# A different projection group first, its weights loaded in halves, and a norm gain spread by matmuls: the start of a hybrid decoder layer

## The chip, the cores and the metric

The kernel runs on one core of one Trainium2 chip. The metric is the device time of one execution in microseconds, as the median of three runs. Before the change it is 636.16 us (635.68 to 637.22).

## The reference, cut to what matters

One decoder layer on x of 512 tokens by 1024 channels, all in float32:

```
hin = rms_norm(x, norm_g[0])
z   = hin @ w_in                 # 1024 x 2964: moba q,k,v; mLSTM q,k,v,o,i,f; NSA q, six k/v, gates
y   = [moba attention | mLSTM * sigmoid(lo) | NSA attention], each head-normalised
x   = x + rms_norm(y @ w_out, norm_g[1])
hm  = rms_norm(x, norm_g[2])
out = x + rms_norm(relu(hm @ w1)**2 @ w2, norm_g[3])
```

Only the first two lines are touched by the change: the norm of x with its gain row `norm_g[0]`, and the order in which the column groups of `w_in` are multiplied. All groups need the whole normalised and transposed x as an operand.

## The kernel before, in words

**Split numbers.** Every large float32 product is made of three matmuls in the fast float32 format (`mm3`, L1614): high part by high part, high by low, low by high. So each weight chunk and each tile of x is first split: ScalarE copies it into a rounded "high" tile (`ring_h`, `xT_h`), and VectorE or GpSimd subtracts that from the original to give the "low" tile (`ring_l`, `xT_l`).

**Weight chunks.** `w_in` comes in chunks of up to 128 x 2048 elements, numbered by `C_...` (L56). SyncE's queue loads them into two buffers `raw[0]` and `raw[1]` (`load_chunk`, L455; a load waits until the chunk two before it has been split), `high_half(c)` on ScalarE (L672) and `low_half(c)` on GpSimd (L600) split them into a ring of three. For chunks 0 and 1 (`SHARED`) VectorE makes the low part of the first half (`chunk_low`, L1113) and GpSimd that of the second.

**Groups and jobs.** Each column group is one or more jobs `J_...` (L61), and a job fills one of eight PSUM banks (its number modulo 8); `READER` says whether VectorE or ScalarE empties it. TensorE runs in a fixed order (L1686 on): `first_group` (group B: 404 mixed columns, the moba and NSA values and gates), the conv groups LQ and LK, LO, the gate transposes, KV, NQ, the gate columns, LV (512 columns, the mLSTM values), MQ, MK, then the attention parts. A token group such as B, LO and LV has the tokens as stationary operand: 4 token tiles x 8 channel blocks x 3 = 96 matmuls, whose moving operand is 404 columns wide for B and 512 for LO and LV. Its two chunks hold channel blocks 0 to 3 and 4 to 7; below, (t,q) is the 12 matmuls of token tile t with chunk q of the group.

**The start.** SyncE issues, in order: x tile 0, the gain row repeated to all 128 partitions (512 KB), chunk 0, x tile 1, chunk 1, x tiles 2 and 3, small parameters, chunk 2. Chunk B is gathered from four column ranges (pieces of 256, 64, 76 and 8 columns). For each token tile: ScalarE takes the sum of squares and a root (`x_root`, L690), VectorE finishes the reciprocal root and multiplies by the gain (`normalise`, L1106, ending at L1110), TensorE transposes eight 128 x 128 blocks into PSUM (`x_transposes`, L1632), ScalarE copies them to `xT_h` (`x_high`, L697) and VectorE makes `xT_l` (`x_low`, L1120). The queues are written out by hand, and the change leaves this order on the two engines as it is:

```
ScalarE: x_root(0) high_half(0) x_high(0) x_root(1) high_half(1) x_root(2) x_high(1) x_root(3) x_high(2) high_half(2) x_high(3)
VectorE: normalise(0) chunk_low(0) x_low(0) normalise(1) chunk_low(1) normalise(2) x_low(1) normalise(3) x_low(2) x_low(3)
TensorE: x_transposes(0) (0,0) x_transposes(1) (0,1) (1,0) x_transposes(2) (1,1) (2,0) x_transposes(3) (2,1) (3,0) (3,1)
```

`x_low` adds 2 to the semaphore `xl_ready` for each tile, and TensorE waits for 2t+2 before tile t's first matmul.

Of the kernel before, what the change touches and what calls it, by code (L numbers as in the profile page):

```python
# [25 lines left out]
F32 = mybir.dt.float32  # L26
# [40 lines left out]
READER = "vvvv" "vvvv" "aaaa" "v" "v" "a" "a" "aa" "a" "vvvv" "aa" "vv" "aaaa" "vv"  # L67

# [70 lines left out]
def ring_previous(c):  # L139

    if C_WO <= c < C_WO + 3:
        return [C_MQ, C_MK, C_LV + 1][c - C_WO]
    return c - 3 if c < C_CMP else c - 4
# [12 lines left out]
def build(nc, x, norm_g, w_in, conv_w, conv_b, gate_b, cmp_pe, cmp_w1, cmp_w2, head_g, w_out, w1, w2, out):  # L156
    ctx = ExitStack()
    with ctx:
# [144 lines left out]
        small_in = sem("small_in")  # L303
        gain0_in = sem("gain0_in")
        gain1_in, gain2_in, gain3_in = sem("gain1_in"), sem("gain2_in"), sem("gain3_in")
# [53 lines left out]
        def released(c):  # L359

            inside = [C_B, C_LO, C_LV, C_WO, C_WO + 1]
# [92 lines left out]
        def _(sp):  # L454
            def load_chunk(c):  # L455
                if c == C_CMP + 2:
                    sp.wait_ge(silu_done, 4)
                elif c == C_CMP + 3:
                    pass
                elif C_WO <= c < C_WO + RAW:  # L460
                    sp.wait_ge(cmp_used, c - C_WO + 1)
                elif c >= RAW:
                    sp.wait_ge(lo_done, split_no(c - RAW) + 1)
                    if c - RAW in SHARED and raw_slot(c) < RAW:
                        sp.wait_ge(lo_first, SHARED.index(c - RAW) + 1)
                view = grid(raw[raw_slot(c)], c)
                parts = chunk_parts(c)[1]
                k0 = 0
                for j, ((n0, n), src) in enumerate(parts):
                    if C_CMP <= c < C_WO:  # L470
                        dst = view[DH * j:DH * j + DH, :, :]
                    elif C_WO <= c:
                        kk = src.shape[1]
                        dst = view[:, k0:k0 + kk, :]
                        k0 += kk
                    else:
                        dst = view[:, :, n0:n0 + n]
                    sp.dma_start(dst, src).then_inc(raw_in[raw_slot(c)], 16)

# [191 lines left out]
        def _(act):  # L671
# [32 lines left out]
            x_root(0)  # L704
            high_half(0)
            x_high(0)
# [7 lines left out]
            x_high(3)  # L714
            high_half(3)

# [12 lines left out]
            for n in range(4):  # L729
                conv_linear(n)  # L730
                if n >= 1:
                    conv_sigmoid(n - 1)
                if n == 1:
                    high_half(4)
            conv_sigmoid(3)
            high_half(5)
            act.wait_ge(read_v, J_B + NT)
            nc.scalar.activation(gt[:], zB[:, :, BG:BG + 12], ACT.Sigmoid).then_inc(gates_ready, 1)
            high_half(6)
# [3 lines left out]
            high_half(7)  # L743

# [20 lines left out]
            act.dma_start(kwinT[0:DH, :], kwinT[DH:P, :]).then_inc(dup_in, 16)  # L765
            high_half(8)
            high_half(9)
            for p in range(2):
# [5 lines left out]
                                 scale=-1.0).then_inc(read_a, 1)  # L774
            high_half(10)
            high_half(11)
# [288 lines left out]
        def _(dve):  # L1065
# [35 lines left out]

            nc.vector.memset(eps1[:], EPS).then_inc(eps_set, 1)
            link(nc.vector.memset(lv1[:, :, :, DV:DV + 1], 1.0))


            def normalise(t):  # L1106
                link(rsqrt1(SS_X + t, R_X + t, ROOT + t, t + 1))
                if t == 0:
                    dve.wait_ge(gain0_in, 16)
                nc.vector.scalar_tensor_tensor(y[:, t, :], xres[:, t, :], stat[:, R_X + t:R_X + t + 1], gain_a[:],  # L1110
                                               ALU.mult, ALU.mult).then_inc(hn_ready, 1)

            def chunk_low(c):  # L1113
                dve.wait_ge(hi_done, split_no(c) + 1)
# [24 lines left out]


            for t in range(NT):
                dve.wait_ge(job_done, J_B + t + 1)
                nc.vector.tensor_copy(zB[:, t, :], ps[:, (J_B + t) % 8, 0:BN]).then_inc(read_v, 1)
# [469 lines left out]
        def _(pe):  # L1613
# [23 lines left out]


            def first_group():

                pe.wait_ge(consts, 2)
                x_transposes(0)
                for t in range(NT):
                    pe.wait_ge(xl_ready, 2 * t + 2)
                    for q in range(2):
                        wh, wl = chunk(C_B + q)
                        for k in range(4):
                            kk = 4 * q + k
                            last = mm3(ps[:, (J_B + t) % 8, 0:BN], xT_h[:, kk, t * P:(t + 1) * P], xT_l[:, kk, t * P:(t + 1) * P],
                                       wh[:, k, :], wl[:, k, :], kk == 0, kk == NC - 1)  # L1650
                        if q == 1:
                            last.then_inc(job_done, 1)
                        elif t == NT - 1:
                            last.then_inc(part_used, 1)
                        if q == 0 and t < NT - 1:
                            x_transposes(t + 1)

# [414 lines left out]
```

## Time and profile before

| what | value |
|---|---|
| median of three runs | 636.16 us (635.68 to 637.22) |
| the profiled execution's own time | 636.81 us |
| its span, first to last instruction | 635.0 us |
| TensorE busy / share of the chain that ended last | 96% / 89% |
| VectorE, ScalarE, GpSimd busy | 61%, 48%, 39% |

The chain that ended last is the sequence of instructions and waits that leads to the end of the kernel without slack; TensorE's matmuls make nearly all of it. Busy time and the chain are given in shares of the span. Times in the timeline count from the first instruction of the span.

### The profile page before, as it was taken

What the parts mean: (1) busy time and instruction counts of PE and PEld (TensorE: products, weight loads), DVE (VectorE), ACT (ScalarE), POOL (GpSimd) and SP (SyncE); (2) the same over time, 40 slices, a digit from 0 to 9 for tenths busy, and PEclk for the clock granted to TensorE, in tenths of its full rate; (3) what the DMA queues carried; (4) which work ended last, traced back from release to release, by engine and by line L of the source; (5) the groups of instructions that cost most, each with busy time, mean ns of one, the idle gap of its engine ahead of it and who ended that gap; (6) DMA issues with size and microseconds to landing.
All of it is one profiled execution on the core that took longest, in us unless ns stands there. A gap on an engine that the chain in (4) does not pass through costs nothing.

```text
span 635.0 us, 8412 instructions
## 1 busy us (share of the span) xinstructions
PE 606.6 (96%) x3172; PEld 499.2 (79%) x3172; DVE 386.8 (61%) x665; ACT 302.1 (48%) x541; POOL 247.4 (39%) x120
## 2 busy tenths in 40 slices
PE   2999999999989989999999999999999999999995
PEld 2988888886876667889987888888888888888884
DVE  4526031104878877288499968569577595681656
ACT  5415264107566974255563564425545445453422
POOL 4422527402526351005336564172533723812611
PEclk9999999999989989999999999999999999999999
DMA  9442449513240222002704353250340613203002
GB/s 281 136 132 68 132 117 233 127 40 116 85 133 10 59 82 85 1 1 67 266 1 165 101 170 96 76 190 2 133 133 2 211 55 132 67 1 126 40 34 100
DMA packets 45724, 63.50 MB, mean 100 GB/s; under 512 B 6616, under 2 KB 34292, under 8 KB 45684
## 3 DMA queue, kind: packets, MB, share of 16 engines
q1 hardware_dynamic: 45524, 62.71, 32.0%
q8 instruction: 25, 0.41, 0.3%
q10 hardware_dynamic: 160, 0.26, 0.2%
q14 instruction: 15, 0.12, 0.1%
HBM read 58.51 MB, written 2.10 MB: 95 GB/s over the span
## 4 chain that ended last, share of the span: by engine, by line
PE 89%; DVE 5%; ACT 2%; issue 1%; DMA 1%; POOL 1%; SPq 0%; DVEq 0%; ACTq 0%
PE ps L1616 20%; PE ps L1617 19%; PE ps L1618 19%; PE ps L2006 7%; PE ps L2008 7%; PE ps L2007 7%; PE ps L1878 2%; PE ps L1758 1%; PE ps L1863 1%; DMA raw<-in_w_in 1%; PE ps L1782 1%; PE ps L1783 1%; DVE stat L1290 1%; DVE probsT L1302 1%; PE ps L1934 1%
## 5 line engine op out<-in xcount | busy, mean ns | idle before, releaser
L1618 PE MATMUL ps<-xT_h,ring_l 128*128 128x512 f32 (+1 forms) x384 | 143.1, 373 | 0.0
L1616 PE MATMUL ps<-xT_h,ring_h 128*128 128x512 f32 (+1 forms) x384 | 143.0, 372 | 0.0
L1617 PE MATMUL ps<-xT_l,ring_h 128*128 128x512 f32 (+1 forms) x384 | 143.0, 372 | 0.0
L661 POOL TENSOR_TENSOR ring_l<-raw_d,ring_h 128x1024 fp32r<-128x1024 f32 x25 | 67.4, 2707 | 130.8 <-ACT ring_h L931 130.8
L661 POOL TENSOR_TENSOR ring_l<-raw,ring_h 128x1024 fp32r<-128x1024 f32 x31 | 76.8, 2502 | 83.9 <-DVE xres L1459 44.4
L604 POOL TENSOR_TENSOR ring_l<-raw,ring_h 128x2048 fp32r<-128x2048 f32 (+1 forms) x16 | 69.5, 4353 | 85.6 <-ACT ring_h L679 85.6
L1553 DVE TENSOR_TENSOR y<-ps,y 128x512 f32<-128x512 f32 x90 | 61.2, 688 | 52.6 <-PE ps L2008 52.2
L1616 PEld LDWEIGHTS ps<-xT_h,ring_h 128*128 128x128 f32 x384 | 72.6, 189 | 12.9
L1617 PEld LDWEIGHTS ps<-xT_l,ring_h 128*128 128x128 f32 x384 | 72.3, 188 | 12.6
L1618 PEld LDWEIGHTS ps<-xT_h,ring_l 128*128 128x128 f32 x384 | 72.3, 188 | 12.6
L2006 PE MATMUL ps<-ring_h,a_h 128*128 128x512 f32 x196 | 77.4, 395 | 0.0
L2008 PE MATMUL ps<-ring_h,a_l 128*128 128x512 f32 x196 | 77.1, 394 | 0.0
L2007 PE MATMUL ps<-ring_l,a_h 128*128 128x512 f32 x196 | 77.0, 393 | 0.0
L1616 PE MATMUL ps<-ring_h,xT_h 128*128 128x512 f32 (+1 forms) x160 | 62.9, 393 | 3.8 <-POOL ring_l L604 3.8
L1617 PE MATMUL ps<-ring_l,xT_h 128*128 128x512 f32 (+1 forms) x160 | 61.8, 386 | 0.0
L1618 PE MATMUL ps<-ring_h,xT_l 128*128 128x512 f32 (+1 forms) x160 | 61.6, 385 | 0.0
L931 ACT ACTIVATE ring_h<-raw 128x1024 fp32r<-128x1024 f32 x32 | 33.1, 1056 | 23.4 <-PE ps L2008 20.2
L2006 PEld LDWEIGHTS ps<-ring_h,a_h 128*128 128x128 f32 x196 | 36.9, 188 | 8.8 <-issue 0.5
L2008 PEld LDWEIGHTS ps<-ring_h,a_l 128*128 128x128 f32 x196 | 36.9, 188 | 8.6
L2007 PEld LDWEIGHTS ps<-ring_l,a_h 128*128 128x128 f32 x196 | 36.9, 188 | 8.4
L968 ACT ACTIVATE ps<-ps 128x512 f32<-128x512 f32 x32 | 18.7, 583 | 50.1 <-PE ps L1618 50.1
L931 ACT ACTIVATE ring_h<-raw_d 128x1024 fp32r<-128x1024 f32 x32 | 33.5, 1054 | 11.6 <-PE ps L2008 10.8
(248 smaller groups left out, 995.5 us busy)
## 6 DMA issues: line engine op xcount, KB each, us to landing
raw<-in_w_mlp SPq DMA_DIRECT2D x16, 1024.0 KB, 5.4
raw_d<-in_w_mlp SPq DMA_DIRECT2D x16, 1024.0 KB, 6.0
raw<-in_w_in SPq DMA_DIRECT2D x9, 1024.0 KB, 5.3
raw<-in_nsa_cmp_w SPq DMA_DIRECT2D x8, 512.0 KB, 7.2
xres<-in_x SPq DMA_DIRECT2D x4, 512.0 KB, 5.9
raw<-in_w_out SPq DMA_DIRECT2D x2, 1024.0 KB, 6.4
raw<-in_w_out SPq DMA_DIRECT2D x4, 512.0 KB, 4.3
out<-xres SPq DMA_DIRECT2D x8, 256.0 KB, 2.1
```

The lines of the kernel that those rows point to most:

```text
L604: nc.gpsimd.tensor_tensor(ring_l[r][:, n0:n], raw[c % RAW][:, n0:n], ring_h[r][:, n0:n].bitcast(F32), ALU.subtract).then_inc(lo_done, 1)
L661: nc.gpsimd.tensor_tensor(slot(ring_l, n), slot_source(n), slot(ring_h, n).bitcast(F32), ALU.subtract).then_inc(lo_done, 1)
L931: nc.scalar.activation(slot(ring_h, n), slot_source(n), ACT.Copy).then_inc(hi_done, 1)
L968: nc.scalar.activation(tile, tile, ACT.Relu).then_inc(relu_ready, 1)
L1553: nc.vector.tensor_tensor(ya, ps[:, product_bank(b, k) + s, :], ya, ALU.add).then_inc(acc_ready, 1)
L1616: nc.tensor.matmul(o, sh, mh, start=start, stop=False)
L1617: nc.tensor.matmul(o, sh, ml, start=False, stop=False)
L1618: return nc.tensor.matmul(o, sl, mh, start=False, stop=stop)
L1878: last = nc.tensor.matmul(ps[DH * m:DH * m + DH, O_BANK[g], j * P:SEQ], zB[:, j, v0:v0 + DH], block_of(pT[:, g % 2], m, slice(j, NT), j), ...
L2006: nc.tensor.matmul(o, ah, wh[:, q, :], start=fresh and q == 0, stop=not fresh, **go_on)
L2007: nc.tensor.matmul(o, ah, wl[:, q, :], start=False, stop=not fresh, **go_on)
L2008: last = nc.tensor.matmul(o, al, wh[:, q, :], start=False, stop=not fresh or q == 1, **go_on)
```

## The change

It does five things. Group LV moves from behind the gate columns to the front, and B becomes the second group. In `first_group` the order is now (0,0) (1,0) (0,1) (1,1) (2,0) (2,1) (3,0) (3,1), with the transposes of the next token tile still behind each (t,0). Chunk 0 (now contiguous rows of 512 columns) is loaded and copied to its high part in two halves. The gain row is loaded once, as 4 KB, and two matmuls with a row of ones spread it to all partitions in PSUM banks 6 and 7, from where `normalise` reads it. TensorE also makes 10 + 8 + 10 transposes of the identity into an unused bank around these steps. Some of ScalarE's `high_half` calls move earlier in its queue, with the numbers of the chunks shifted, and the parameter transposes go to another bank.

```diff
-C_B, C_LQ, C_LK, C_LO, C_KVS, C_NQ, C_LV, C_MQ, C_MK, C_CMP, C_WO, C_MLP = 0, 2, 3, 4, 6, 7, 8, 10, 11, 12, 16, 20
+C_LV, C_B, C_LQ, C_LK, C_LO, C_KVS, C_NQ, C_MQ, C_MK, C_CMP, C_WO, C_MLP = 0, 2, 4, 5, 6, 8, 9, 10, 11, 12, 16, 20
-J_B, J_CONV, J_LO, J_LI, J_LF, J_KV, J_KS, J_NQ, J_GC, J_LV, J_MQ, J_MK, J_MB, J_H = (
-    0, 4, 8, 12, 13, 14, 15, 16, 18, 19, 23, 25, 27, 31)
+J_LV, J_B, J_CONV, J_LO, J_LI, J_LF, J_KV, J_KS, J_NQ, J_GC, J_MQ, J_MK, J_MB, J_H = (
+    0, 4, 8, 12, 16, 17, 18, 19, 20, 22, 23, 25, 27, 31)
-PARAM_BANK = 7
+PARAM_BANK = 3
+WARM = (10, 8, 10)
...
+                    if c == 0:
+                        sp.dma_start(dst[:, 0:2, :], src[:, 0:2, :]).then_inc(first_in, 16)
+                        dst, src = dst[:, 2:4, :], src[:, 2:4, :]
                     sp.dma_start(dst, src).then_inc(raw_in[raw_slot(c)], 16)
...
-            sp.dma_start(gain_a[:], norm_g[0, 0:1, :].to_broadcast([P, D])).then_inc(gain0_in, 16)
+            sp.dma_start(gain_a[0:1, :], norm_g[0, 0:1, :]).then_inc(gain0_in, 16)
...
             x_root(0)
-            high_half(0)
+            act.wait_ge(first_in, 16)
+            nc.scalar.activation(ring_h[0][:, 0:CHUNK // 2], raw[0][:, 0:CHUNK // 2], ACT.Copy).then_inc(first_hi, 1)
+            act.wait_ge(raw_in[0], raw_full(0))
+            nc.scalar.activation(ring_h[0][:, CHUNK // 2:], raw[0][:, CHUNK // 2:], ACT.Copy).then_inc(hi_done, 1)
             x_high(0)
...
                 if t == 0:
-                    dve.wait_ge(gain0_in, 16)
-                nc.vector.scalar_tensor_tensor(y[:, t, :], xres[:, t, :], stat[:, R_X + t:R_X + t + 1], gain_a[:],
+                    dve.wait_ge(gain0_wide, 1)
+                nc.vector.scalar_tensor_tensor(y[:, t, :], xres[:, t, :], stat[:, R_X + t:R_X + t + 1],
+                                               ps[:, 6:8, :].rearrange("p b n -> p (b n)"),
                                                ALU.mult, ALU.mult).then_inc(hn_ready, 1)
...
+            def warm(n):
+                for _ in range(n):
+                    nc.tensor.transpose(ps[:, 5, 0:P], ident[:], ident[:])
             def first_group():
                 pe.wait_ge(consts, 2)
+                warm(WARM[0])
+                pe.wait_ge(ones_set, 1)
+                pe.wait_ge(gain0_in, 16)
+                for b in range(2):
+                    last = nc.tensor.matmul(ps[:, 6 + b, :], ones_row[:], gain_a[0:1, 512 * b:512 * b + 512], start=True, stop=True)
+                last.then_inc(gain0_wide, 1)
+                warm(WARM[1])
                 x_transposes(0)
-                for t in range(NT):
-                    pe.wait_ge(xl_ready, 2 * t + 2)
-                    for q in range(2):
-                        wh, wl = chunk(C_B + q)
+                warm(WARM[2])
+                for t, q in [(0, 0), (1, 0), (0, 1), (1, 1), (2, 0), (2, 1), (3, 0), (3, 1)]:
+                    if q == 0:
+                        pe.wait_ge(xl_ready, 2 * t + 2)
+                    if t == 0 and q == 0:
+                        pe.wait_ge(lo_first, 1)
+                        wh, wl = grid(ring_h[0], C_LV), grid(ring_l[0], C_LV)
+                    else:
+                        wh, wl = chunk(C_LV + q)
+                    for k in range(4):
+                        kk = 4 * q + k
+                        if t == 0 and kk == 2:
+                            pe.wait_ge(lo_done, 1)
...
             first_group()
+            token_group(J_B, C_B, BN)
...
-            token_group(J_LV, C_LV, 512)
```

## Rows read from the trace of the kernel before

**Rows 1.** The page: engine busy time and the chain that ended last, by engine.

```profile
PE 606.6 (96%) x3172; PEld 499.2 (79%) x3172; DVE 386.8 (61%) x665; ACT 302.1 (48%) x541; POOL 247.4 (39%) x120
...
PE 89%; DVE 5%; ACT 2%; issue 1%; DMA 1%; POOL 1%; SPq 0%; DVEq 0%; ACTq 0%
```

**Rows 2.** TensorE's waits, 0 to 200 us: total us, times, longest.

```profile
PE ps L1635 <- DVE y L1110: 8.1, 1, 8.1
PE ps L1616 <- POOL ring_l L604: 3.8, 1, 3.8
```

**Rows 3.** Timeline of token tile 0: start us, us, engine, line, what.

```profile
1.23 0.29 POOL L578 TENSOR_SCALAR_AFFINE_SELECT ident<-ident 128x128 f32<-128x128 f32 x1 [0.23 <-POOL ident L576]
...
4.22 1.06 ACT L692 ACTIVATE junk<-xres 128x1024 f32<-128x1024 f32 x1 [1.92 <-DMA xres<-in_x]
...
6.64 1.28 DVE L1110 SCALAR_TENSOR_TENSOR y<-xres,stat,gain_a 128x1024 f32<-128x1024 f32 x1
...
8.08 1.94 PE L1635 MATMUL ps<-ident,y 128*128 128x128 f32 x8 [8.08 <-DVE y L1110]
9.34 1.55 ACT L679 ACTIVATE ring_h<-raw 128x1616 fp32r<-128x1616 f32 x1 [3.64 <-DMA raw<-in_w_in]
...
10.80 1.06 ACT L700 ACTIVATE xT_h<-ps 128x512 fp32r<-128x512 f32 x2
...
10.97 2.71 POOL L604 TENSOR_TENSOR ring_l<-raw,ring_h 128x808 fp32r<-128x808 f32 x1 [6.53 <-ACT ring_h L679]
...
13.78 0.68 PE L1616 MATMUL ps<-ring_h,xT_h 128*128 128x404 f32 x1 [3.77 <-POOL ring_l L604]
```

**Rows 4.** Timeline: TensorE's steps at 404 columns, early and later.

```profile
16.95 0.54 PE L1616 MATMUL ps<-ring_h,xT_h 128*128 128x404 f32 x1
...
17.28 0.54 PE L1617 MATMUL ps<-ring_l,xT_h 128*128 128x404 f32 x1
...
22.66 0.35 PE L1616 MATMUL ps<-ring_h,xT_h 128*128 128x404 f32 x1
...
22.85 0.34 PE L1617 MATMUL ps<-ring_l,xT_h 128*128 128x404 f32 x1
...
23.22 1.03 PE L1635 MATMUL ps<-ident,y 128*128 128x128 f32 x8
```

**Rows 5.** Timeline: chunk 1 and the x tiles behind it, ScalarE and VectorE.

```profile
12.93 0.29 ACT L687 ACTIVATE stat<-stat,eps 128x1 f32<-128x1 f32 x1
...
13.76 1.55 ACT L679 ACTIVATE ring_h<-raw 128x1616 fp32r<-128x1616 f32 x1 [0.53 <-DMA raw<-in_w_in]
...
14.09 1.28 DVE L1110 SCALAR_TENSOR_TENSOR y<-xres,stat,gain_a 128x1024 f32<-128x1024 f32 x1
...
15.55 1.06 ACT L692 ACTIVATE junk<-xres 128x1024 f32<-128x1024 f32 x1 [0.24 <-DMA xres<-in_x]
...
16.73 0.30 ACT L687 ACTIVATE stat<-stat,eps 128x1 f32<-128x1 f32 x1
...
19.56 1.29 DVE L1123 TENSOR_TENSOR xT_l<-ps,xT_h 128x512 fp32r<-128x512 f32 x2
...
25.26 1.92 ACT L679 ACTIVATE ring_h<-raw 128x2048 fp32r<-128x2048 f32 x1
```

**Rows 6.** Stretches of the span, TensorE: length, busy (count), granted clock, DMA share, GB/s.

```profile
13.78:17.86 4.08, 4.08 (x12) 1.00 1.04 355
20.93:36.23 15.30, 15.30 (x90) 1.00 0.34 112
36.46:58.30 21.84, 21.84 (x98) 1.00 0.18 51
103.54:125.40 21.86, 21.86 (x97) 1.00 0.61 162
```

**Rows 7.** Stretches: length, PE, PEld, DVE, ACT, POOL busy, granted clock, DMA, GB/s.

```profile
154.00:155.00 1.00, 0.29 (x3) 0.29 (x3) 0.00 (x0) 0.97 (x5) 0.16 (x2) 1.00 1.14 160
...
158.00:159.00 1.00, 1.00 (x9) 0.78 (x6) 0.90 (x5) 0.67 (x3) 0.24 (x1) 0.50 1.04 401
```

**Rows 8.** Timeline: two stretches of plain float32 matmuls on TensorE.

```profile
158.64 2.09 PE L1758 MATMUL ps<-lv,probsT 128*128 128x129 f32 x8
...
165.56 2.05 PE L1758 MATMUL ps<-lv,probsT 128*128 128x129 f32 x16 [0.56 <-DVE probsT L1302]
```

More of the change, by code:

```diff
@@ L53 @@
 RAW = 2
-C_B, C_LQ, C_LK, C_LO, C_KVS, C_NQ, C_LV, C_MQ, C_MK, C_CMP, C_WO, C_MLP = 0, 2, 3, 4, 6, 7, 8, 10, 11, 12, 16, 20
+C_LV, C_B, C_LQ, C_LK, C_LO, C_KVS, C_NQ, C_MQ, C_MK, C_CMP, C_WO, C_MLP = 0, 2, 4, 5, 6, 8, 9, 10, 11, 12, 16, 20
 FB = 4
 NB = FF // P // FB
-J_B, J_CONV, J_LO, J_LI, J_LF, J_KV, J_KS, J_NQ, J_GC, J_LV, J_MQ, J_MK, J_MB, J_H = (
-    0, 4, 8, 12, 13, 14, 15, 16, 18, 19, 23, 25, 27, 31)
+J_LV, J_B, J_CONV, J_LO, J_LI, J_LF, J_KV, J_KS, J_NQ, J_GC, J_MQ, J_MK, J_MB, J_H = (
+    0, 4, 8, 12, 16, 17, 18, 19, 20, 22, 23, 25, 27, 31)
 NJOB = 33
 HT_BANK = 4
-PARAM_BANK = 7
-READER = "vvvv" "vvvv" "aaaa" "v" "v" "a" "a" "aa" "a" "vvvv" "aa" "vv" "aaaa" "vv"
+PARAM_BANK = 3
+WARM = (10, 8, 10)
+READER = "vvvv" "vvvv" "vvvv" "aaaa" "v" "v" "a" "a" "aa" "a" "aa" "vv" "aaaa" "vv"
 K_ORDER = [2, 3, 4, 5, 6, 7, 0, 1]
@@ L141, in ring_previous @@
     if C_WO <= c < C_WO + 3:
-        return [C_MQ, C_MK, C_LV + 1][c - C_WO]
+        return [C_MQ, C_MK, C_NQ][c - C_WO]
     return c - 3 if c < C_CMP else c - 4
@@ L241, in build @@
         oT = at("oT", [P, SEQ], F32, o_p + 6144)
+        ones_row = at("ones_row", [1, P], F32, o_p)
         blk = at("blk", [P, CMP_LEN, NP_], F32, o_p + 8192)
@@ L303, in build @@
         small_in = sem("small_in")
-        gain0_in = sem("gain0_in")
+        gain0_in, gain0_wide = sem("gain0_in"), sem("gain0_wide")
+        first_in, first_hi, ones_set = sem("first_in"), sem("first_hi"), sem("ones_set")
         gain1_in, gain2_in, gain3_in = sem("gain1_in"), sem("gain2_in"), sem("gain3_in")
@@ L359, in released @@
         def released(c):
-            inside = [C_B, C_LO, C_LV, C_WO, C_WO + 1]
+            inside = [C_LV, C_B, C_LO, C_WO, C_WO + 1]
             if c in inside:
@@ L714, in _ @@
             x_high(3)
-            high_half(3)
+            for c in (3, 4, 5, 6):
+                high_half(c)
             def conv_linear(n):
@@ L733, in _ @@
                 if n == 1:
-                    high_half(4)
+                    high_half(7)
             conv_sigmoid(3)
-            high_half(5)
-            act.wait_ge(read_v, J_B + NT)
+            act.wait_ge(*reads(J_B + NT - 1))
             nc.scalar.activation(gt[:], zB[:, :, BG:BG + 12], ACT.Sigmoid).then_inc(gates_ready, 1)
-            high_half(6)
+            high_half(8)
             for t in range(NT):
@@ L742, in _ @@
                 nc.scalar.activation(y[:, t, 256:768], ps[:, (J_LO + t) % 8, :], ACT.Sigmoid).then_inc(read_a, 1)
-            high_half(7)
+            high_half(9)
             act.wait_ge(job_done, J_LF + 1)
@@ L765, in _ @@
             act.dma_start(kwinT[0:DH, :], kwinT[DH:P, :]).then_inc(dup_in, 16)
-            high_half(8)
-            high_half(9)
+            high_half(10)
             for p in range(2):
@@ L774, in _ @@
                                  scale=-1.0).then_inc(read_a, 1)
-            high_half(10)
             high_half(11)
@@ L1102, in _ @@
             nc.vector.memset(eps1[:], EPS).then_inc(eps_set, 1)
+            nc.vector.memset(ones_row[:], 1.0).then_inc(ones_set, 1)
             link(nc.vector.memset(lv1[:, :, :, DV:DV + 1], 1.0))
@@ L1108, in normalise @@
                 if t == 0:
-                    dve.wait_ge(gain0_in, 16)
-                nc.vector.scalar_tensor_tensor(y[:, t, :], xres[:, t, :], stat[:, R_X + t:R_X + t + 1], gain_a[:],
+                    dve.wait_ge(gain0_wide, 1)
+                nc.vector.scalar_tensor_tensor(y[:, t, :], xres[:, t, :], stat[:, R_X + t:R_X + t + 1],
+                                               ps[:, 6:8, :].rearrange("p b n -> p (b n)"),
                                                ALU.mult, ALU.mult).then_inc(hn_ready, 1)
             def chunk_low(c):
-                dve.wait_ge(hi_done, split_no(c) + 1)
+                dve.wait_ge(first_hi, 1) if c == 0 else dve.wait_ge(hi_done, split_no(c) + 1)
                 n = size(c) // 2
@@ L1137, in _ @@
             x_low(3)
+            for t in range(NT):
+                dve.wait_ge(job_done, J_LV + t + 1)
+                nc.vector.tensor_copy(lv1[:, t, :, 0:DV], ps[:, (J_LV + t) % 8, :].rearrange("p (h d) -> p h d", h=HEADS)
+                                      ).then_inc(read_v, 1)
             for t in range(NT):
@@ L1188, in _ @@
             nc.vector.tensor_tensor(m_split[:, 1, :], g_row[:, 2, :], m_split[:, 0, :].bitcast(F32), ALU.subtract).then_inc(m_ready, 1)
-            for t in range(NT):
-                dve.wait_ge(job_done, J_LV + t + 1)
-                nc.vector.tensor_copy(lv1[:, t, :, 0:DV], ps[:, (J_LV + t) % 8, :].rearrange("p (h d) -> p h d", h=HEADS)
-                                      ).then_inc(read_v, 1)
             for p in range(2):
@@ L1636, in x_transposes @@
                 last.then_inc(xt_done, 1)
+            def warm(n):
+                for _ in range(n):
+                    nc.tensor.transpose(ps[:, 5, 0:P], ident[:], ident[:])
             def first_group():
                 pe.wait_ge(consts, 2)
-                x_transposes(0)
-                for t in range(NT):
-                    pe.wait_ge(xl_ready, 2 * t + 2)
-                    for q in range(2):
-                        wh, wl = chunk(C_B + q)
[L1647 to L1656, printed above, removed]
+                warm(WARM[0])
[5 more added lines that the diff above has]
+                warm(WARM[1])
+                x_transposes(0)
+                warm(WARM[2])
[11 more added lines that the diff above has]
+                            pe.wait_ge(lo_done, 1)
+                        last = mm3(ps[:, (J_LV + t) % 8, :], xT_h[:, kk, t * P:(t + 1) * P], xT_l[:, kk, t * P:(t + 1) * P],
+                                   wh[:, k, :], wl[:, k, :], kk == 0, kk == NC - 1)
+                    if q == 1:
+                        last.then_inc(job_done, 1)
+                    elif t == NT - 1:
+                        last.then_inc(part_used, 1)
+                    if q == 0 and t < NT - 1:
+                        x_transposes(t + 1)
@@ L1678, in feature_group @@
                     bank_free(j0 + j)
-                    if j0 + j == PARAM_BANK:
+                    if j0 + j == J_CONV + PARAM_BANK:
                         pe.wait_ge(params_ready, 2)
@@ L1686, in _ @@
             first_group()
+            token_group(J_B, C_B, BN)
             pe.wait_ge(consts, 13)
             pe.wait_ge(small_in, 16 * 8)
+            pe.wait_ge(*reads(J_LV + PARAM_BANK))
             nc.tensor.transpose(ps[:, PARAM_BANK, 0:28], rows[:], ident[0:28, 0:28])
@@ L1693, in _ @@
             token_group(J_LO, C_LO, 512)
-            pe.wait_ge(read_v, J_B + NT)
+            pe.wait_ge(*reads(J_B + NT - 1))
             for job, b0 in ((J_LI, BI), (J_LF, BF)):
```

## The prediction, made before the changed kernel was run

> **What bounds the kernel now.** I read the page first: TensorE is busy for 96% of the span and holds 89% of the chain that ended last [rows 1]. Then TensorE's waits in the first 200 us: 8.1 us until the first normalised tile, 3.8 us until the low part of chunk 0, and nothing else before the attention parts [rows 2]. From 20.93 us on it is busy for the whole of every stretch of the projections [rows 6]. So the only time that the change can win or lose lies before about 21 us, and what I have to find is when TensorE has finished groups LV and B together. In the kernel before, B ends at 36.23 and LV costs 21.86 us wherever it stands [rows 6], so the mark is 36.23 + 21.86 = 58.1 us; all later work is the same and needs nothing that is late (ring, buffers and readers move with the groups, and one 512-column group of 21.84 us covers the 1.92 us copies and the GpSimd halves of its chunks several times over).
>
> Before the mark, three things cost time. Tile 0 is normalised at 7.92, transposed by 10.02, and the matmuls start only at 13.78, held by GpSimd's low half of chunk 0 [rows 3]. The granted clock reads 1.00 in these rows, but the steps of 404 columns are 0.33 us apart at 17 us and 0.19 us at 22.7 us [rows 4]: TensorE ran at the 1.2 GHz level up to about 17.6 us, in spite of the column. Twelve matmuls took 4.08 us [rows 6], against 12 x 0.19 = 2.3: 1.8 us lost.
>
> **The change, part by part.**
>
> *Loads.* The 512 KB broadcast and the gathered chunk go; a row of 4 KB and two contiguous halves of 512 KB come. Up to the end of chunk 1 the queue carried 512 + 512 + 808 + 512 + 808 = 3152 KB before, landing at 13.74, just ahead of the copy that waited for it [rows 5]. After it is 512 + 4 + 1024 + 512 + 1024 = 3076 KB: at the same pace 13.4 us; at the pace of the fastest microseconds (401 GB/s, rows 7, against 355 in this stretch, rows 6) about 12. I take 12.9. Chunk 0's halves land at about 6.1 and 7.7, by the same pace, after tile 0 at 4.2 [rows 3]. The Trainium skill, in "DMA: Bandwidth & Descriptors", section Specifications, says that pieces under 512 bytes lose line rate; by it the old chunk with its 32-, 256- and 304-byte pieces was slow and the new order would be at the fast end, near 12. The trace leaves this open, since its fast microseconds have other loads in them.
>
> *Gain by matmuls.* `normalise(0)` was ready at 6.64 and now waits for them. The row lands no earlier than tile 0, about 4.2 to 4.6. The two matmuls are plain float32 with 512 columns. No row has that shape. A plain float32 call leaves two records; with 129 columns 16 records take 2.05 us at the full clock and 8 take 2.09 at half clock [rows 8], so 129 columns cost 0.26 or 0.52 a call, and scaled to 512 both calls together 2.0 or 4.1 us. These are upper ends, since the load of the stationary operand is in them and doesn't grow with the columns; the lower end is a call as cheap as a step of 512 columns in the fast format, 0.23 (21.86 / 96, rows 6). The spread gain is ready between 4.7 and 8.7. I take 7.2, nearest to the scaled rows, with part of the work at either clock. A gain in time is excluded: the statistics themselves are only ready at 6.64. At 8.7 it would cost 2.1 on tile 0, and 1 on the end (through A, below). Reading the gain from PSUM costs nothing to 0.15 us on 1.28. Cost on tile 0: 0.6 us.
>
> *Dummy transposes.* Identity is ready at 1.52 [rows 3]. At about 0.2 us each the first ten fill up to 3.6, all in front of work that isn't there yet. They cost nothing unless they run into `x_transposes(0)`; the middle eight end about 1 us behind the gain matmuls, at 8.2, and tile 0 is ready at 8.5. With the clock up, the tile's eight transposes take 1.03 as at 23.22 instead of 1.94 [rows 3, 4].
>
> *Tile 0's start.* Normalised 8.55, transposed 9.75. ScalarE's copy of the second half is done by about 9 (two copies of about 1.06, one after the other), so `x_high(0)` is no longer queued behind a 1.55 us copy: 9.75 + 1.1 = 10.85, and `x_low(0)` is done 0.85 later, 11.7. GpSimd's half of chunk 0, 1024 elements by 2.71 x 1024/808 = 3.4, ends near 12.4, and TensorE needs it only half way through (0,0). So the first matmul comes at 11.7 instead of 13.78: 2.1 us won, and 1.8 more if the clock is up.
>
> *What is late next.* (0,0) takes 12 x 0.228 = 2.7 us (96 matmuls in 21.86, rows 6), the transposes of tile 1 some 0.8: TensorE has nothing at 15.3. The new order asks for (1,0), so for `x_low(1)`, and on VectorE that stands behind `chunk_low(1)` and `normalise(2)`, which needs `x_root(2)`, which on ScalarE stands behind `high_half(1)`, which waits for chunk 1. Call A the start of that copy. It is the later of chunk 1's landing (12.9) and the end of `x_root(1)`, 10.85 + 1.5 = 12.35 (1.48 from 15.55 to 17.03, rows 5). From A: copy of 2048 elements 1.92; `x_root(2)` 1.48; from the root to the end of `normalise` 13.22 to 15.37 = 2.15; `x_low` 1.29 [rows 5]; with gaps 6.9. So `x_low(1)` is ready at S = 19.8 us. Before, it was ready at 20.85 [rows 5], but TensorE had had (0,0) and (0,1) to do until 20.9 and waited for nothing. (0,1) could run at A + 1.92 + 3.4 = 18.2, but the written order puts it behind (1,0). TensorE idles for about 4.5 us.
>
> *The sum.* After S there remain 84 matmuls of LV at 0.228 = 19.1, two sets of transposes at 0.8 = 1.6, B's 96 at 0.184 = 17.7, and 0.2 of gaps: 38.6. The end of both groups is 19.8 + 38.6 = 58.4, against 58.1: +0.3 us. The won start is given back whole, because 12 matmuls that used to fill the wait now come after it.
>
> *The clock again.* Where TensorE was busy 0.29 us in the microsecond at 154, the granted clock stood at 0.50 four microseconds later, at the 1.2 GHz level, with TensorE fully busy again [rows 7]. An idle stretch of 4.5 us is longer than that one. One spell at the low level costs up to 1.8 us, as at the start; nothing, if it doesn't fall. Some of the spell may lie in the idle time. I take 1.5. Total +1.8 us on the profiled span (635.0 to 636.8; the time around the span is 636.81 - 635.0 = 1.8 us more, and this execution lies 0.65 above the median). On the median: 636.16 + 1.8 = 637.9 us.
>
> **The rivals.** A measurement of this kernel tells from no change what exceeds 0.3%, 1.9 us.
>
> Forecast, chance 0.49: stall behind (1,0), and one low spell of the clock. With A between 12.35 and 13.5 and 1.2 to 1.8 for the clock, +1.0 to +2.8: 637.2 to 638.9.
>
> The dummy work doesn't raise the clock, 0.17. Nothing in this trace speaks for or against: the eight transposes at 8.08 were over after 1.94 us. Then the gain is ready at 7.9, tile 0 normalised 9.2, transposed 11.2, `x_low(0)` 13.1, `x_root(1)` 13.8; (0,0) runs to about 18, `x_low(1)` is ready near 21 and the idle time shrinks to 1.5 us, with no fall behind it: 21 + 38.6 = 59.6, +1.5, 637.7. This is what the Trainium skill, "TensorE: Matmul & The Clock Gate", Part 4, says: transposes don't count as activity for the clock.
>
> The clock is up and stays up, 0.12: +0.3, and -0.8 if chunk 1 is early: 635.4 to 636.5. Against it is the fall near 158.
>
> Slower beyond doubt, 0.10: the clock falls and stays low for a second spell, because the rest of the stall lies in it or the wait for tile 2 follows. Each further spell costs 1.8: 58.4 + 1.5 + 1.8, +3.6, 639.8. It decides if more than 1.9 us of matmul time is lost at the low level.
>
> Faster by over 1.9 us, 0.12: `x_low(1)` would have to be ready at 17.9 without a fall, A at 11.0. `x_high(0)` alone ends at 10.2 at best, and `x_root(1)` adds 1.5, so the early part can't give it; only if also the fall near 158 is escaped by other timing (1.6 us) does it come to -2.4 with the early landing.
>
> **How the numbers follow.** In the forecast case somewhat under half of the weight, 0.23, lies above 638.07. Slower: 0.23 + 0.10 for the long low spell + 0.02 from the cold start with a late gain = 0.35. Faster is its rival alone, 0.12. The rest, 0.53, is within 0.3%. The range takes the forecast, the cold start and most of the case without a fall, and stops short of two full spells: 635.2 to 639.5. The likeliest case's own range is 637.2 to 638.9.
>
> **What would show it.** In the new profile: first LV matmul near 11.7 with steps of 0.23 us; a wait of TensorE of 3 to 5 us on `xT_l` that ends near 19.8; steps of 0.43 us or a granted clock of 0.50 behind it; the end of B at 58 to 61; from there everything shifted by one amount. Wrong if chunk 1's copy starts before 12, if no wait stands before (1,0), or if the later stages move by an amount of their own.

## The result, and the profile after

The changed kernel takes 641.1 us (median of 6 runs, 639.6 to 643.19) against 635.84 us for the kernel before in the same comparison (6 runs, 635.02 to 637.22): a ratio of 1.0087, 95% interval 1.0068 to 1.0107. It is slower by 5.3 us from median to median, 5.5 by the ratio. I had forecast 637.9 us and given a range up to 639.5.

The profiled execution took 640.09 us with a span of 638.3. First the page: engine busy time and the chain by engine, to be held against [rows 1].

```profile
PE 614.2 (96%) x3204; PEld 504.2 (79%) x3204; DVE 388.1 (61%) x666; ACT 302.1 (47%) x542; POOL 246.3 (39%) x120
...
PE 89%; DVE 6%; ACT 3%; issue 1%; POOL 0%; DVEq 0%; POOLq 0%; ACTq 0%
```

TensorE is 7.6 us busier, with 28 dummy transposes and 2 small matmuls more, and still makes 89% of the chain. Busy time doesn't tell useful work from slow or idle work; the waits do. The largest of TensorE in the first 200 us, which stand where [rows 2] stood:

```profile
PE ps L1625 <- DVE xT_l L1132: 5.0, 1, 5.0
PE ps L1787 <- DVE probsT L1311: 3.2, 4, 1.6
PE ps L1651 <- POOL ident L584: 1.6, 1, 1.6
```

The two early waits of 8.1 and 3.8 us are gone, and one of 5.0 us has come: the first matmul of the second token tile waits for that tile's low part. The timeline of all engines around it, answering to [rows 3, 5]:

```profile
1.58 2.40 PE L1651 MATMUL ps<-ident 128*128 128x128 f32 x10 [1.58 <-POOL ident L584]
...
4.08 3.75 PE L1660 MATMUL ps<-gain_a,ones_row 1*128 1x512 f32 x4
...
7.94 1.28 DVE L1118 SCALAR_TENSOR_TENSOR y<-xres,stat,ps 128x1024 f32<-128x1024 f32 x1 [1.20 <-PE ps L1660]
...
9.52 1.92 PE L1644 MATMUL ps<-ident,y 128*128 128x128 f32 x8
...
11.22 2.34 PE L1651 MATMUL ps<-ident 128*128 128x128 f32 x10
...
13.44 0.66 PE L1625 MATMUL ps<-ring_h,xT_h 128*128 128x512 f32 x1
...
13.82 1.90 ACT L685 ACTIVATE ring_h<-raw 128x2048 fp32r<-128x2048 f32 x1
...
15.80 2.38 POOL L610 TENSOR_TENSOR ring_l<-raw,ring_h 128x1024 fp32r<-128x1024 f32 x1 [3.22 <-ACT ring_h L685]
...
15.98 3.27 DVE L1126 TENSOR_TENSOR ring_l<-raw,ring_h 128x1024 fp32r<-128x1024 f32 x1
...
16.48 1.03 PE L1644 MATMUL ps<-ident,y 128*128 128x128 f32 x8
...
21.20 1.28 DVE L1132 TENSOR_TENSOR xT_l<-ps,xT_h 128x512 fp32r<-128x512 f32 x2
...
22.54 0.79 PE L1625 MATMUL ps<-ring_h,xT_h 128*128 128x512 f32 x1 [5.02 <-DVE xT_l L1132]
...
24.41 0.63 PE L1626 MATMUL ps<-ring_l,xT_h 128*128 128x512 f32 x1
...
24.84 0.63 PE L1627 MATMUL ps<-ring_h,xT_l 128*128 128x512 f32 x1
```

Read from the left: the gain matmuls hold the normalising of tile 0 until 7.94; its transposes take 1.92 us, still at the low clock; the first matmul comes at 13.44, only 0.34 us earlier than before. Tile 1 is transposed by 17.5, but its low part is ready only at 22.48, because VectorE is held for 3.27 us by a subtraction that takes 1.22 elsewhere. Then the steps of (1,0) are 0.43 us apart. The stretches show what the granted clock did in the wait and behind it (columns as in [rows 7]):

```profile
19.00:20.00 1.00, 0.00 (x0) 0.00 (x0) 0.86 (x5) 0.97 (x3) 0.00 (x0) 1.00 0.00 0
20.00:21.00 1.00, 0.00 (x0) 0.00 (x0) 1.00 (x1) 0.00 (x0) 0.00 (x0) 0.83 0.62 62
...
26.00:27.00 1.00, 1.00 (x4) 0.71 (x4) 0.00 (x0) 0.00 (x0) 0.00 (x0) 0.50 0.00 0
...
28.00:29.00 1.00, 1.00 (x9) 0.92 (x8) 0.00 (x0) 0.26 (x1) 0.00 (x0) 1.00 0.00 0
```

The clock fell within the wait: 0.83 between 20 and 21 us puts the fall near 20.7. It came back at about 27.5, when nearly all of (1,0) had run at 1.2 GHz. Group B's last matmul starts at 63.20 and ends about 0.2 later, 63.4, where the sum for the kernel before gives 58.1: +5.3 us. The matmuls at the end of all the projections start at 152.7 instead of 147.2: +5.5, as large as the difference of the medians. I call that moment the mark; the runs below are read by it too. Behind it, the profiled execution got 2.2 us back (its span is only 3.3 longer): the granted clock fell once behind the mark (near 171), and three times in the profiled execution before (near 158, 178 and 229). That differs from execution to execution, and whether the change has a part in it isn't shown: its six runs have mean clocks of 0.989 (three, 639.8 us on average) or 0.982 to 0.983 (three, 642.6).

### The profile page after: what moved, and what is told of

It is laid out like the page before. It is cut to its first block, busy times and chain, and to the rows that moved or that the text cites. A ratio compares the mean times of both kernels' runs of the same rounds, so it can differ in the third digit from the quotient of the medians.

```text
span 638.3 us, 8481 instructions
## 1 busy us (share of the span) xinstructions
PE 614.2 (96%) x3204; PEld 504.2 (79%) x3204; DVE 388.1 (61%) x666; ACT 302.1 (47%) x542; POOL 246.3 (39%) x120
## 4 chain that ended last, share of the span: by engine, by line
PE 89%; DVE 6%; ACT 3%; issue 1%; POOL 0%; DVEq 0%; POOLq 0%; ACTq 0%
PE ps L1625 19%; PE ps L1626 19%; PE ps L1627 19%; PE ps L2035 7%; PE ps L2037 7%; PE ps L2036 7%; PE ps L1907 2%; PE ps L1892 1%; ACT W L802 1%; PE ps L1787 1%; PE ps L1651 1%; PE ps L1811 1%; DVE stat L1299 1%; DVE probsT L1311 1%; PE ps L1660 1%
## 5 line engine op out<-in xcount | busy, mean ns | idle before, releaser
L610 POOL TENSOR_TENSOR ring_l<-raw,ring_h 128x2048 fp32r<-128x2048 f32 (+2 forms) x16 | 67.9, 4249 | 104.3 <-ACT ring_h L685 99.4
L1625 PEld LDWEIGHTS ps<-xT_h,ring_h 128*128 128x128 f32 x384 | 72.6, 189 | 12.9
L1625 PEld LDWEIGHTS ps<-ring_h,xT_h 128*128 128x128 f32 x160 | 30.7, 192 | 10.6 <-DVE xT_l L1132 5.5
```

The source lines that it names most:

```text
L610: nc.gpsimd.tensor_tensor(ring_l[r][:, n0:n], raw[c % RAW][:, n0:n], ring_h[r][:, n0:n].bitcast(F32), ALU.subtract).then_inc(lo_done, 1)
L1625: nc.tensor.matmul(o, sh, mh, start=start, stop=False)
```

## The experiments

All times below are medians beside the kernel before on the same chip, whose medians were 635.2 to 635.3 (635.84 for the changed kernel's row). What came back is the difference of two ratios. The last two columns are of one profiled execution each: TensorE's longest wait behind (0,0), and the mark. That execution is not the median one: it was the slowest of its runs for e1_order, e4_gain_dma and e7_fill, and the fastest for e12_queues_nowarm.

| run | median us | ratio, 95% interval | wait, us | mark, us |
|---|---|---|---|---|
| kernel before | 635.3 | 1 | none | 147.2 |
| changed kernel | 641.1 | 1.0087 (1.0068 to 1.0107) | 5.0 | 152.7 |
| e1_order | 635.69 | 1.0011 (0.999 to 1.0032) | 1.9 | 148.9 |
| e2_queues | 634.78 | 0.9985 (0.9969 to 1.0002) | 2.0 | 147.8 |
| e3_nowarm | 639.02 | 1.0048 (1.0032 to 1.0064) | 3.1 | 150.4 |
| e4_gain_dma | 638.6 | 1.0054 (1.0034 to 1.0075) | 5.3 | 152.4 |
| e5_queues_gain_dma | 634.74 | 0.9988 (0.9972 to 1.0003) | 2.0 | 146.5 |
| e6_pool_later | 636.88 | 1.0033 (1.0014 to 1.0052) | 3.2 | 149.7 |
| e7_fill | 638.46 | 1.005 (1.0029 to 1.0072) | filled | 150.6 |
| e8_before_order | 639.17 | 1.0052 (1.0036 to 1.0067) | 2.0 | 151.6 |
| e9_before_warm | 635.15 | 0.9998 (0.9987 to 1.0009) | 0.5 | 147.8 |
| e10_before_warm_queues | 638.9 | 1.0048 (1.0028 to 1.0067) | 3.0 | 150.1 |
| e11_filled | 635.27 | 0.9996 (0.9979 to 1.0012) | filled | 146.6 |
| e12_queues_nowarm | 637.5 | 1.0036 (1.0023 to 1.005) | 2.0 | 147.9 |

Theory 1 was that of the prediction: the wait for tile 1, with a fall of the clock behind it, because nothing stands before (1,0) in TensorE's order. The rivals were that the gain matmuls, the dummies or the loads cost the time.

**The order alone, taken back (e1_order).**

```diff
-for t, q in [(0, 0), (1, 0), (0, 1), (1, 1), (2, 0), (2, 1), (3, 0), (3, 1)]:
+for t, q in [(0, 0), (0, 1), (1, 0), (1, 1), (2, 0), (2, 1), (3, 0), (3, 1)]:
```

> The changed kernel with one edit: (0,1) comes before (1,0), as in the kernel before. Theory 1 (TensorE waits 5.0 us for the low part of token tile 1 and then runs a low spell of the clock, because nothing else is ordered before it): (0,1) can start when the low halves of chunk 1 are there, about 19.3 us, ends at 22.0, (1,0) follows at 22.5; the wait shrinks to about 1.8 us, 2.7 us of matmuls are saved, and the 2.4 us of half-clock steps go too if the idle time is now too short for a fall: 3 to 5 us less than the changed kernel, 636 to 638.5. Rival (the time is lost in the gain matmuls, the dummy transposes or the loads): no more than 1 us comes back, 640 to 641.

0.76% came back, 4.8 of the 5.5 us. The timeline of e1_order shows the one wait left in this stage, in front of (0,1) for VectorE's half of chunk 1. In this execution the clock fell all the same, near 21 us; it was the slowest of twelve that reach from 634.45 (mean clock 0.994) to 639.31 (0.985).

```profile
19.44 0.47 PE L1625 MATMUL ps<-ring_h,xT_h 128*128 128x512 f32 x1 [1.92 <-DVE ring_l L1126]
21.11 0.63 PE L1625 MATMUL ps<-ring_h,xT_h 128*128 128x512 f32 x1
```

**Tile 1 made ready earlier, order kept (e2_queues).**

```diff
 ScalarE:
-x_root(2)
 x_high(1)
+x_root(2)
 VectorE:
-chunk_low(1)
-normalise(2)
 x_low(1)
+chunk_low(1)
+normalise(2)
```

> The changed kernel with the order of (1,0) and (0,1) kept, but ScalarE copies token tile 1 before it takes the root of tile 2, and VectorE makes the low part of tile 1 before the low half of chunk 1 and before normalising tile 2. Theory 1: tile 1 is ready at about 19.4 instead of 22.5, so the wait of TensorE is 2 us instead of 5.0: 3 us less, and up to 5 if the clock doesn't fall, 636 to 638. Rival (the lateness of tile 1 isn't what costs the time; something later takes it back): 640 to 641.

1.02% came back, 6.5 us. TensorE's timeline of e2_queues: tile 1 at 19.60 instead of 22.54, and steps at the full clock behind it.

```profile
19.60 0.50 PE L1625 MATMUL ps<-ring_h,xT_h 128*128 128x512 f32 x1 [2.01 <-DVE xT_l L1132]
```

Two edits that have nothing in common but that wait both take the loss away. With that the rival falls as the main cause; what the dummies and the gain matmuls cost beside it is the matter of e3_nowarm and e4_gain_dma.

**The order alone, in the kernel before (e8_before_order).** `first_group` of the kernel before, with the new list of (t,q) and group B still first.

> The kernel before with the new order of the steps alone: (0,0) (1,0) (0,1) (1,1) and on, group B still first. Theory 1 (the order alone makes TensorE wait for tile 1): (0,1), 2.2 us, no longer fills the time until tile 1's low part is ready at 20.85, so TensorE waits 2.2 us and the end comes 2.2 us later, more if the clock falls: 637.5 to 639.5 where the kernel before has 635.3. Rival (the order is harmless, the group or the loads cost the time): 635.3.

It made 0.52%, 3.3 us, slower. TensorE's waits of e8_before_order in the first 60 us have one more than [rows 2]:

```profile
PE ps L1616 <- DVE xT_l L1123: 2.0, 1, 2.0
```

The wait is 2.0 us; from 22.7 to 25 us the steps behind it were 0.34 apart instead of 0.18, one more low spell.

**Without the dummies (e3_nowarm).** `WARM = (0, 0, 0)`.

> The changed kernel without its 28 dummy transposes. If the dummies raise the clock for (0,0): its 12 steps go from 0.23 to 0.43 us, (0,0) ends 2.4 us later, inside the wait for tile 1, so the end of the kernel hardly moves (at most 0.5 us later), and the clock may even not fall afterwards (2 us earlier). If the dummies do nothing: the steps of (0,0) stay as they are and the time is 641 again. If they delay the gain matmuls or tile 0: tile 0 is normalised earlier than 7.94.

0.4% faster than with them, 2.5 us, the case with no fall. TensorE's timeline of e3_nowarm: the first eight steps of (0,0) ran at the low clock, 0.43 a step (15.21 is its fourth), and so it ended 1.8 us later; the wait was 3.1 us, and (1,0) behind it ran at 0.23 a step (23.28 is its fourth).

```profile
13.77 0.80 PE L1625 MATMUL ps<-ring_h,xT_h 128*128 128x512 f32 x1 [2.38 <-DVE xT_l L1132]
...
15.21 0.63 PE L1625 MATMUL ps<-ring_h,xT_h 128*128 128x512 f32 x1
...
22.48 0.50 PE L1625 MATMUL ps<-ring_h,xT_h 128*128 128x512 f32 x1 [3.13 <-DVE xT_l L1132]
...
23.28 0.40 PE L1625 MATMUL ps<-ring_h,xT_h 128*128 128x512 f32 x1
```

The dummies made (0,0) fast, so that TensorE stood idle for longer, 5.0 us, and the clock that they had raised fell. That the length of the wait decides it is the likely reading, not a shown one: in the profiled execution of e1_order the clock fell behind a wait of 1.9 us, in that of e2_queues it stayed up behind one of 2.0.

**The wait filled (e7_fill).** `if t == 1 and q == 0: warm(40)` stands ahead of the wait for tile 1.

> The changed kernel with 40 more dummy transposes in front of (1,0), where TensorE waited for 5.0 us. If transposes keep the clock up: the steps of (1,0) stay at 0.23 us instead of 0.43, 2.4 us come back, 638 to 639 where the kernel before has 635.3; the wait itself stays. If they don't count as activity (as the Trainium skill says in TensorE: Matmul & The Clock Gate, Part 4): steps of 0.43 us and 640 to 641 as in the changed kernel, or up to 1 us more if the dummies run past the end of the wait at half speed.

0.37% came back, 2.4 us. The stretches of e7_fill, first the 40 dummies, then (1,0): the granted clock stays at 1.00, and 12 matmuls take 2.86 us where the changed kernel's took 5.1.

```profile
17.35:21.88 4.53, 4.53 (x42) 4.29 (x40) 4.39 (x7) 2.42 (x5) 1.01 (x1) 1.00 0.45 99
22.71:25.57 2.86, 2.86 (x12) 2.32 (x13) 1.83 (x5) 0.00 (x0) 0.00 (x0) 1.00 0.49 93
```

This prices the fall at 2.4 us by the medians and 2.3 by these rows, and shows that transposes alone keep the clock up. The Trainium skill says in "TensorE: Matmul & The Clock Gate", Part 4, that transposes don't count as busy for the clock; these rows are against it, for float32 transposes of 128 x 128.

**GpSimd's half of chunk 1 later (e6_pool_later).** In `low_half` stands `if c == 1: pool.wait_ge(hn_ready, 3)`, so that GpSimd waits until tile 2 is normalised.

> The changed kernel with one wait more: GpSimd makes its half of chunk 1's low part only after token tile 2 is normalised. Theory (VectorE's half of chunk 1 took 3.27 us instead of 1.22 because GpSimd had begun its own half of the same subtraction 0.2 us earlier, and the two don't run side by side): VectorE's half takes 1.2 us, tile 1's low part is ready at about 20.4 instead of 22.5, TensorE's wait falls from 5.0 to 3.0 us: 2.1 us less, up to 4.5 less if the clock doesn't fall; 636.5 to 639 where the kernel before has 635.3. Rival (VectorE was slow for another reason, such as the loads or ScalarE): its half still takes 3.2 us, and the time stays at 640 to 641.

The timeline of e6_pool_later: VectorE's half takes 1.22 us again, and x_low(1) comes 2.3 us earlier than in the changed kernel.

```profile
15.71 1.22 DVE L1128 TENSOR_TENSOR ring_l<-raw,ring_h 128x1024 fp32r<-128x1024 f32 x1
...
18.88 1.28 DVE L1134 TENSOR_TENSOR xT_l<-ps,xT_h 128x512 fp32r<-128x512 f32 x2
...
19.11 2.37 POOL L612 TENSOR_TENSOR ring_l<-raw,ring_h 128x1024 fp32r<-128x1024 f32 x1 [6.49 <-DVE y L1120]
```

0.54% came back, 3.4 us, although the clock fell behind the wait here too (steps of 0.43 us from 21.1 to 24.1). In the changed kernel GpSimd's half ran from 15.80 to 18.18 and VectorE's from 15.98 to 19.25: 2.2 us of waiting, then 1.1 of work. The Trainium skill, "SBUF — State Buffer", section "SBUF: two separate sides", gives the rule: VectorE with two SBUF inputs and GpSimd share a port pair, whoever starts first holds it for its whole instruction, and the other is blocked. The trace agrees, with 3.27 against 1.22 us.

**The gain by its load (e4_gain_dma).** The broadcast load is back, the gain matmuls are gone.

> The changed kernel with the gain row broadcast by its load again, as before, and no gain matmuls. The gain matmuls took 3.75 us and delayed the start of normalising tile 0 from about 6.8 to 7.94. With them gone tile 0 starts 1.2 us earlier if the 512 KB more in the queue don't delay the halves of chunk 0; chunk 1 lands about 1.6 us later and delays the chain to tile 1 by 0.5 to 1 us. Theory 1 (only the chain to tile 1 counts): 0 to 1 us more than the changed kernel. Rival (the gain matmuls are on the path): 1.2 us less.

0.33% faster, 2.1 us, so neither number was right; the two intervals overlap. The timeline of e4_gain_dma:

```profile
13.54 1.92 ACT L685 ACTIVATE ring_h<-raw 128x2048 fp32r<-128x2048 f32 x1 [0.60 <-DMA raw<-in_w_in]
...
15.49 1.23 DVE L1126 TENSOR_TENSOR ring_l<-raw,ring_h 128x1024 fp32r<-128x1024 f32 x1 [0.40 <-ACT ring_h L685]
15.53 3.38 POOL L610 TENSOR_TENSOR ring_l<-raw,ring_h 128x1024 fp32r<-128x1024 f32 x1 [2.47 <-ACT ring_h L685]
...
17.24 1.70 DVE L1106 SCALAR_TENSOR_TENSOR stat<-stat 128x1 f32<-128x1 f32 x1
```

The gain matmuls were on the path: without them `x_root(1)` ended 1.0 us earlier, at 12.94. But the larger load took most of that back, since chunk 1's copy now waited 0.60 us for it and started at 13.54 instead of 13.82. (1,0) came 0.84 us earlier, at 21.70, and the mark only 0.3; the rest of the 2.1 us of the medians isn't in this profile. Here VectorE began its half first and GpSimd lost the microsecond; then an operation on one column, normally 0.22 us, was held to 1.70 by what was left of GpSimd's.

**The candidates.** e5_queues_gain_dma joins e2_queues and e4_gain_dma. e11_filled adds dummies in its idle stretches, and e12_queues_nowarm leaves all dummies out.

> The changed kernel with tile 1 ahead in ScalarE's and VectorE's order (as in the run that did that alone, 0.9985 of the kernel before) and the gain row broadcast by its load. With the gain matmuls gone the first projection matmul came at 12.46 instead of 13.44, and tile 1's transposes ended 1.1 us earlier. If the start now follows tile 1: (1,0) starts at about 18.3 instead of 19.6, and 1.0 to 1.3 us come off, a ratio of 0.996 to 0.997. If something else holds the start (the larger load makes chunk 1 late, GpSimd's half of chunk 1 holds VectorE): no change against 0.9985.

> The candidate for the best version: the changed kernel with tile 1 ahead in the two queues and the gain row broadcast by its load (0.9988 of the kernel before), and the idle stretches of TensorE filled with dummy transposes: 24 at the start, 14 before (0,0), 14 before (1,0). Half of the executions without the fill had a mean granted clock of 0.989 and 635.5 us, the others 0.992 and 634.2. If the idle stretches make the difference, all go to the higher clock: 633.5 to 634.3, a ratio of 0.997 to 0.998. Rival (the spells of low clock come from the attention part): 634.7 as without the fill.

> The changed kernel with tile 1 ahead in the two queues and the gain row broadcast by its load (0.9988 of the kernel before), now without any dummy transposes. There TensorE no longer waits long for tile 1, so a cold start is on its path: the 12 steps of (0,0) at 0.43 us instead of 0.23 end 2.4 us later, tile 1's transposes and copies behind them too, and (1,0) starts at about 20.5 instead of 18.25. If so the end is 2 to 2.5 us later, 636.8 to 637.3 where the kernel before has 635.3, unlike the changed kernel as it was, where leaving the dummies out made it 2 us faster. Rival (the dummies are worth nothing anywhere): 634.7.

(1,0) came at 18.25 in e5_queues_gain_dma and the mark at 146.5, 1.3 us before that of e2_queues, as expected. The ratio isn't the expected 0.996 to 0.997: the medians of the two can't be told apart, nor from the kernel before (0.9988, up to 1.0003). Filling the idle stretches won nothing (0.9996): the spells of low clock that remained in its profiled execution lie near 150 and 167 us, in the attention part. Without the dummies it is 0.48% slower than e5_queues_gain_dma, 3.0 us: where TensorE doesn't wait long anyway, a cold start is on its path. The timeline of e12_queues_nowarm has steps of 0.43 at 13.8, and tile 1 at 19.65 instead of 18.25:

```profile
12.34 0.80 PE L1625 MATMUL ps<-ring_h,xT_h 128*128 128x512 f32 x1 [2.29 <-DVE xT_l L1132]
...
13.79 0.63 PE L1625 MATMUL ps<-ring_h,xT_h 128*128 128x512 f32 x1
...
19.65 0.50 PE L1625 MATMUL ps<-ring_h,xT_h 128*128 128x512 f32 x1 [2.01 <-DVE xT_l L1132]
```

That is 1.4 us at the start and at the mark, and the two profiled executions are 1.5 apart (635.27 and 633.8). The medians say 3.0: the other five executions of e12_queues_nowarm had a lower mean clock (0.987 to 0.992, against 0.994), and no profile shows where.

**The dummies in the kernel before (e9_before_warm, e10_before_warm_queues).** 34 transposes of the identity ahead of tile 0's, 22 behind them.

> The kernel before with dummy transposes alone: 34 ahead of the first token tile's transposes, from 1.6 us on, and 22 behind them, in front of the first projection matmul. If transposes raise the clock, the steps of (0,0) are 0.19 us apart instead of 0.34 and TensorE finishes them 1.8 us earlier; but tile 1's low part hangs on chunk 1 (13.76) and its chain, so it is ready at 20.8 as before and nearly nothing is won: 634.8 to 635.5 where the kernel before has 635.3. If the clock isn't raised: the steps stay at 0.34, and the 34 dummies at 0.2 us end at 8.4, 0.3 us late: up to 1 us slower. Rival (the cold start is on the path): 1.8 us less.

> The same dummies in the kernel before, and tile 1 ahead of chunk 1's low half and of token tile 2 in ScalarE's and VectorE's order. Tile 1's low part is then ready at about 19.0, (0,1) waits for GpSimd's half of chunk 1 until 18.1 and ends at 20.3, and (1,0) follows without a wait: about 0.6 us less than the kernel before, 634.5 to 635.

e9_before_warm is the same as the kernel before. Its timeline shows a clock that came and went: the 34 dummies at 0.2 us each, tile 0's transposes at the full clock, and after 2.4 us of idle time (0,0) again at 0.34 a step. So this profile doesn't show the fast (0,0) that the run was made for. The profile of e10_before_warm_queues does, with the same dummies and the same 2.4 us of idle time: the fall isn't the same in every execution.

```profile
1.58 6.70 PE L1642 MATMUL ps<-ident 128*128 128x128 f32 x34 [1.58 <-POOL ident L578]
...
8.12 1.04 PE L1635 MATMUL ps<-ident,y 128*128 128x128 f32 x8
...
13.98 0.55 PE L1616 MATMUL ps<-ring_h,xT_h 128*128 128x404 f32 x1 [2.42 <-POOL ring_l L604]
```

e10_before_warm_queues had the fast (0,0), and I had it wrong by 4 us: (0,1) needs VectorE's half of chunk 1 too, and my edit had put that half behind tile 1. TensorE's waits of e10_before_warm_queues:

```profile
PE ps L1616 <- DVE ring_l L1117: 3.0, 1, 3.0
```

What one order of VectorE gives to (1,0) it takes from (0,1). The order of an engine's work has to fit TensorE's, which is the fault of the change itself.

## Why the prediction was wrong

The place and the mechanism were right; three sizes were too small, and they all fell on the same side. The step that failed most is the term for `chunk_low(1)` in the chain from A to tile 1's low part: the sum put it at nothing, beside `x_root(2)`, and it took 3.27 us.

- **Tile 0's start:** 11.7 forecast, 13.44 measured. The gain was ready at 7.83, not 7.2 (the two calls took 3.75 us, inside the bounds, but at the low clock throughout; reading it from PSUM cost nothing, 1.28 us as before), and tile 0's transposes took 1.92, not 1.03. What failed here is "with the clock up": after 8 us of TensorE work, dummies and one-row matmuls, the clock was still at 1.2 GHz. It was up for (0,0), so the rival of a cold start held for tile 0's transposes and not for the matmuls.
- **A, the copy of chunk 1:** 12.9 forecast, 13.82 measured, +0.9. It started right behind `x_root(1)`, which is late with tile 0; the load, of which the trace has a landing 9.2 us behind its issue at 3.06, near 12.3, was not what held it.
- **From A to tile 1's low part:** 6.9 forecast, 8.66 measured, +1.8, the largest term. The working put `chunk_low(1)` beside `x_root(2)` and so at nothing, and named no price for the case that this cover is gone. It took 3.27 us, since GpSimd's half of the same chunk had begun 0.2 us before. The trace of the kernel before was there to be asked: in [rows 3] GpSimd's half of chunk 0 takes 2.71 us for 808 elements, where 2048 take 4.61 with VectorE idle, which gives 1.8 for 808, and the other 0.9 is what was left of VectorE's half. One of VectorE's small operations, normally 0.22 us, took 0.68 there, up to the end of GpSimd's half of chunk 1 at 18.12. I scaled the 2.71 up to 3.4 and did not ask what made it long, nor who would have to wait when the two start the other way round. The two rows, from the timeline of the kernel before:

```profile
17.45 0.68 DVE L1099 SCALAR_TENSOR_TENSOR stat<-stat 128x1 f32<-128x1 f32 x1
...
27.25 4.61 POOL L604 TENSOR_TENSOR ring_l<-raw,ring_h 128x2048 fp32r<-128x2048 f32 x1 [9.14 <-ACT ring_h L679]
```

- **The wait and the clock:** 4.5 us of idle time forecast, 5.0 measured; the clock fell as forecast, at a price of 2.3 (12 steps at 0.43 instead of 0.23), not 1.5. +0.8.
- **After S:** 38.6 us forecast, and from 22.5 to 63.4 it is 40.9, less 2.3 for the clock 38.6. Right.

0.9 + 1.8 + 0.8 = 3.5, which with the 1.8 forecast makes the 5.3 found at the end of group B: 3.0 of waiting and 2.3 of low clock. The text says that "the won start is given back whole"; in fact there was almost no start won.

What was right: the only place that counts lies before (1,0); the order (0,1) after (1,0) is what gives it away (e1_order, e8_before_order); the chain through VectorE and ScalarE sets it (e2_queues); the later stages move by one amount up to the mark. The rival "slower beyond doubt" was to be told by more than 1.9 us lost at the low level, and 2.3 were: the clock stayed low for 6.8 us, from 20.7 to 27.5. By that sign it came true in part. But its sum, +3.6, has 3.3 of clock in it and nothing of the longer chain, so that it comes nearer to the measured time than the forecast partly by luck. In the rival "faster" there is a slip: `x_low(1)` at 17.9 gives 17.9 + 38.6 = 56.5, which is 1.6 before 58.1 and not 1.9.

Left open: what sets the spells of low clock in the attention part, which move single executions by 2 us and more, and whether group LV in front, or chunk 0 in two halves, is worth anything by itself. No run does either alone; the best ones with it (0.9985, 0.9988) have intervals that touch no change.

## What to carry to other kernels

When a step is moved ahead in the order of the engine that bounds the kernel, look for what it waits for through the hand-written queues of all other engines, and for what used to fill that time. A faster start is worth nothing if the next thing that it needs isn't earlier too; keeping the engine's clock up pays where it isn't about to wait long. Where it is, filling the wait as well (e7_fill, 1.005) came to the same as leaving the dummies out (e3_nowarm, 1.0048). Two halves of one subtraction given to VectorE and GpSimd did not run side by side here; put the one that others wait for first, or give the other a reason to start later.

## What the runs showed of the hardware that I had not expected

- A subtraction of two SBUF tiles on VectorE took 1.22 us with GpSimd idle and 3.27 when GpSimd had begun one of its own 0.2 us earlier; even an operation on one column, with two inputs in SBUF, went from 0.22 to 1.70 us.
- Float32 transposes keep TensorE at the 2.4 GHz level (e7_fill: 1.00 through 4.5 us of them) and raise it (e9_before_warm: up by 8.1 us, with nothing but 34 of them before, since tile 0's eight then took 1.04). In the changed kernel, with matmuls of one row for 3.75 us in between, it was still at 1.2 GHz 9.9 us after the first dummy: tile 0's eight took 1.92. Whether the one-row matmuls are the reason isn't isolated.
- The granted clock's column reads 1.00 from the start of the span until the first fall, whatever the level is: in the changed kernel it does so at 9.52 to 11.44 us, where eight transposes took 1.92 us instead of 1.03. Only the spacing of the instructions tells the level there.
- The clock doesn't move alike where TensorE has done the same: behind 56 dummies, tile 0's transposes and 2.4 us of idle time (0,0) ran at 0.34 a step in the profile of e9_before_warm and at 0.18 in that of e10_before_warm_queues.
